# Splitting the first table load in two and spreading the decay rates by TensorE

## Chip, cores and metric

The kernel runs on one core of a Trainium2 chip, as one launch. The metric is the device time of one execution in microseconds, as a median over runs. All data are float32.

## What is computed

Two transformer blocks follow one another for one sequence of 256 tokens and width 1024. The first has a mixer of two parts (a bidirectional mLSTM and a Hyena long convolution), then a mixture of 16 experts; the second, of two layers over latent and context tokens, is not touched. The part that the change touches is the start of the first block: the modulation from `c`, the norm of `x`, and the Hyena filters with their window.

```
mod = (c @ w_ada[l] + b_ada[l])[:, None, :]
h = rms_norm(x, g_mix[l]) * (1 + sc1) + sh1
...
hid = jnp.sin(fr * (z @ w1.astype(f32) + b1.astype(f32)))
hid = jnp.sin(fr * (hid @ w2.astype(f32) + b2.astype(f32)))
h = hid @ w3.astype(f32)
window = jnp.exp(-t * jnp.abs(deltas.astype(f32))) + HYENA_WINDOW_SHIFT
return (h * window).reshape(L, HYENA_ORDER, HYENA_DIRS, HYENA_WIDTH)
```

`deltas` (the decay rates) are 2048 numbers: two orders by two directions by 512 channels. Each is the same for all 256 positions. The filters then go through a Fourier transform, are multiplied with the signal's, and come back.

## The kernel before, in words

Every engine has its own instruction stream, written out by hand in program order; semaphores join them. PE is TensorE, ACT ScalarE, DVE VectorE, POOL GpSimd, SP the engine that issues all DMAs. A stream waits where `wait_ge` stands, and what is behind waits too.

**SP and the ring.** SP issues first the small inputs (L2989 to L2991: the Hyena MLP's weights, its features, the parameter columns), then the tables `tab` (L2992, one transfer of 128 x 2878), the decay rates `dlt` (L2993, the 2048 numbers copied to all 128 partitions) and `x` (L2994). Then come the weights, by `load`, in the order of the list `stream`: slots of up to 2 MB in a ring that holds four. The first slots are `ada0` to `ada4` (parts of the modulation weights `w_ada`, issued at L3005), then `z`, `x1`, `q` and so on (parts of `w_in`). A slot's transfer waits until PE has used what lay in its place, so `ada4` waits for `ada0`. Between the fourth and the fifth slot SP issues four small transfers (L3009 to L3012), counted by `rows_loaded` (`s_row`). Semaphore `tables_loaded` (`s_load`) counts tables and rates, 16 each.

**PE at the start.** Two hidden layers of the Hyena MLP (L1287, L1291, each with a sine by ACT behind it), four filter products (L1298, 64 rows of weights by 512 columns, for order 0), one modulation slot (`ada()`, L1255: `ada0`), four filter products for order 1, the sums of the squares of `x` (L1281, from `sums`), slot `ada1`, the Fourier products of order 0 (`spectrum(0)`, L1311), slots `ada2`, `ada3` and `ada4` with the turning of the first modulation rows behind the last (L1272), `spectrum(1)`, and then the projections `z`, `x1` and so on (L1236). Results go to PSUM banks; `open_bank` takes them in turn from a ring of seven (`MIX_BANKS`) and waits until the last user of a bank has freed it.

**ACT and DVE at the start.** ACT makes the windows, `exp(-t * rate)`, eight of 128 x 512 (L1634 by way of the helper's L1605): `minus_t` is a column of `tab`, the rates are read from SBUF. DVE adds 0.05 and multiplies with the filter (L1842), then forms sum and difference of both directions (L1844, L1845). DVE frees a window for ACT by `window_used`. POOL squares `x` (L2924).

Tables, by columns of `tab`: `ident`, `ones`, then masks for the mLSTM (`tri`, `neg`), the forward Fourier tables (`dft`), the inverse ones (`idft`), 544 columns of zeros named `unused` (the place is overwritten later on), and 30 columns of small things (`minus_t`, `eps`, `pick` and others).

Of the kernel before, what the change touches and what calls it, by code (L numbers as in the profile page):

```python
# [15 lines left out]
ACT = mybir.ActivationFunctionType  # L16
# [3 lines left out]
P = 128  # L20
# [4 lines left out]
W = 512  # L25
# [13 lines left out]
MIX_BANKS, ADA_BANKS = (0, 1, 2, 3, 4, 5, 6), (7,)  # L39
# [18 lines left out]
def offsets(parts):  # L58
    at, out = 0, {}
    for name, width in parts:  # L60
# [3 lines left out]

TABLES1 = [("ident", 128), ("ones", 128), ("tri_f", 128), ("tri_b", 128), ("neg_f", 128), ("neg_b", 128),
           ("dft_c", 256), ("dft_s", 256), ("idft_c", 512), ("idft_s", 512), ("unused", 544),
           ("minus_t", 2), ("eps", 1), ("ln_eps", 1), ("pick", 8), ("token", 2), ("fold", 16)]
TABLES2 = [("half64", 128), ("flip64", 128), ("neg_col", 64), ("rope_c", 256), ("rope_s", 256),  # L70
           ("rope_r", 128), ("gla_lv", 160), ("diag32", 32), ("gla_bd", 256)]
# [91 lines left out]
def build(nc, I, out):  # L163
    ctx = ExitStack()
    with ctx:
# [7 lines left out]
        tcol, n_tab = offsets(TABLES1)  # L173
# [4 lines left out]
        tab = sb("tab", [P, n_tab])  # L178
# [17 lines left out]
        def tb(name):  # L196
            return tab[:, slice(*tcol[name])]

        ident, ones = tb("ident"), tb("ones")
# [22 lines left out]
        dlt = at(14376, 4 * W)  # L222
# [8 lines left out]
        win = [at(23600, W), at(25136, W)]  # L231
# [113 lines left out]
        def open_bank(pe, name, banks=ALL_BANKS):  # L345

            assert name not in place, name
            n = turn_of[banks] = turn_of.get(banks, -1) + 1
            b = banks[n % len(banks)]
            use = uses[b]  # L350
            uses[b] += 1
            place[name] = (b, use)
            if use:
                pe.wait_ge(free[b], use)
            return ps[b]

        def close_bank(ins, name):

            ins.then_inc(full[place[name][0]], 1)

        def read_bank(eng, name):

            b, use = place[name]
            eng.wait_ge(full[b], use + 1)
            return ps[b]
# [29 lines left out]
        s_load = sem("tables_loaded")  # L395
# [3 lines left out]
        s_row = sem("rows_loaded")  # L399
# [3 lines left out]
        hid_ready = sem("hid_ready")  # L403
        arg_ready = sem("sine_argument_ready")
        win_ready, win_used = sem("window_ready"), sem("window_used")
# [87 lines left out]
        slots, start = [{}, {}], 0  # L493
# [710 lines left out]
        def _(pe):  # L1204
            mm = nc.tensor.matmul
# [80 lines left out]
            b = open_bank(pe, "hid1", MIX_BANKS)  # L1286
# [2 lines left out]
            pe.wait_ge(hid_ready, 1)  # L1289
            b = open_bank(pe, "hid2", MIX_BANKS)  # L1290
            close_bank(mm(b[0:64, 0:T], hw2[0:64, :], hid[0:64, :], start=True, stop=True), "hid2")  # L1291
            pe.wait_ge(hid_ready, 2)
            for o in range(2):
                for n in range(TT):
                    for d in range(2):
                        j = 2 * o + d
                        b = open_bank(pe, f"filt{o}{n}{d}", MIX_BANKS)
                        close_bank(mm(b[:], hid2[0:64, P * n:P * n + P], w3[0:64, W * j:W * j + W],  # L1298
                                       start=True, stop=True), f"filt{o}{n}{d}")
                if o == 0:  # L1300
                    ada()
            pe.wait_ge(s_load, 32)
            sums("ss0", sq0, sq0_ready)
            ada()

# [72 lines left out]
            pe.wait_ge(ht_scaled, 1)  # L1378
            project("z")
            project("x1")  # L1380
            pe.wait_ge(s_row, 64)
            by_groups("gates", wg)
            w = take("q")
            fmajor("q0", w, 0, lambda k: hT[:, k, :])
# [5 lines left out]
            b = open_bank(pe, "F", MIX_BANKS)  # L1390
            for t in range(TT):
                for d in range(2):
                    o = b[:, 8 * t + 4 * d:8 * t + 4 * d + 4]
# [11 lines left out]
            for t in range(TT):  # L1405
                b = open_bank(pe, f"v{t}", MIX_BANKS)
# [16 lines left out]
            for h in range(H):  # L1423
                b = open_bank(pe, f"s{h}", MIX_BANKS)
# [4 lines left out]
            for c in range(2):  # L1429
                b = open_bank(pe, f"hss{c}", MIX_BANKS)  # L1430
# [3 lines left out]
            for d in range(2):  # L1434
                for t in range(TT):
                    for hp in range(2):
                        b = open_bank(pe, f"num{d}{t}{hp}", MIX_BANKS)
# [9 lines left out]
            for t in range(TT):  # L1447
                b = open_bank(pe, f"ym{t}", MIX_BANKS)
# [13 lines left out]
            b = open_bank(pe, "ss1", MIX_BANKS)  # L1462
# [140 lines left out]
        def act_mixers(act, step, tell):  # L1603
            def a(out_, in_, f, **kw):
                return nc.scalar.activation(out_, in_, f, **kw)  # L1605
# [17 lines left out]
            for i in range(2):  # L1623
                act.wait_ge(arg_ready, i + 1)
                step(a((hid, hid2)[i][0:64, :], hid2[0:64, :], ACT.Sin), hid_ready)
            act.wait_ge(s_load, 32)
            for o in range(2):
                for n in range(TT):
                    for d in range(2):
                        j = 2 * o + d  # L1630
                        k = (o * TT + n) * 2 + d
                        if k > 1:
                            act.wait_ge(win_used, k - 1)
                        step(a(win[d], dlt[:, W * j:W * j + W], ACT.Exp, scale=tb("minus_t")[:, n:n + 1]), win_ready)  # L1634

            def root(name, out_, n, k):
                read_bank(act, name)
# [155 lines left out]
        def dve_mixers(dve, step, tell):  # L1793
# [23 lines left out]
            for i in range(2):  # L1817
# [13 lines left out]
                if i == 0:  # L1831
                    dve.wait_ge(s_fil, 48)
                    step(v.tensor_copy(cpad[:, :, 0], pc("c", 0, 8)), c_ready)
            dve.wait_ge(s_load, 32)
            for o in range(2):
                for n in range(TT):
                    for d in range(2):
# [36 lines left out]
            tell(h_ready)  # L1874
            spectrum(1)
            T1v = T1.rearrange("p (a b) -> p a b", b=T)
            dve.wait_ge(s_row, 64)
            step(v.memset(vtok, 1.0))

            def conv(dst, src, wname, bname, m, n):  # L1880
# [1040 lines left out]
        def pool_mixers(pool, step, tell):  # L2921
            g = nc.gpsimd
            pool.wait_ge(s_x, 16)
            step(g.tensor_tensor(sq0, xT, xT, ALU.mult), sq0_ready)  # L2924
            pool.wait_ge(s_load, 32)
            for c, first in enumerate((8, 0, 4)):
                pool.wait_ge(hx_evac, c + 1)
                for m in range(first, first + 4):
                    x, y, tmp = hxc[:, m, :], hxp[:, (m + 4) % 12, :], rs
                    step(g.tensor_scalar(x, y[:, 0:T], pc("conv_hy_w", m), pc("conv_hy_b", m), ALU.mult, ALU.add))  # L2930
                    for j in (1, 2):
                        step(g.tensor_scalar(tmp, y[:, j:j + T], pc("conv_hy_w", 12 * j + m), None, ALU.mult))
                        step(g.tensor_tensor(x, x, tmp, ALU.add))
                tell(hc_ready)
# [52 lines left out]
        def _(sp):  # L2987
            for dst, src in ((hw1[0:33, :], I["hy_w1"][0]), (hfe[0:33, :], I["features"]), (hhp[0:64, 0:3], I["hy_cols"])):
                sp.dma_start(dst, src).then_inc(s_hid, 16)  # L2989
            for dst, src in ((hw2[0:64, :], I["hy_w2"][0]), (w3[0:64, :], I["hy_w3"][0]), (par[:], I["params"])):  # L2990
                sp.dma_start(dst, src).then_inc(s_fil, 16)  # L2991
            sp.dma_start(tab[:], I["tables1"]).then_inc(s_load, 16)  # L2992
            sp.dma_start(dlt, I["hy_deltas"].to_broadcast([P, 4 * W])).then_inc(s_load, 16)  # L2993
            sp.dma_start(xT, I["xT"].rearrange("(k p) t -> p k t", p=P)).then_inc(s_x, 16)  # L2994

            def load(n):
                name, src = stream[n]
                if after[n] >= 0:
                    sp.wait_ge(*freed[after[n]])
                v = slot(n, src)  # L3000
                if name[:2] == "fi":
                    for h in range(2):
                        sp.dma_start(v[:, :, 256 * h:256 * h + 256], src[:, :, h, :]).then_inc(landed[n % LANES], 16)
                else:
                    sp.dma_start(v, src).then_inc(landed[n % LANES], 16)  # L3005

            for n in range(4):
                load(n)
            sp.dma_start(bv, I["b_v"].to_broadcast([P, W])).then_inc(s_row, 16)  # L3009
            sp.dma_start(bg, I["b_gates"].to_broadcast([P, NG])).then_inc(s_row, 16)  # L3010
            sp.dma_start(wg, I["w_gates"].rearrange("p (k n) -> p k n", k=KD)).then_inc(s_row, 16)
# [98 lines left out]
```

## Time and profile before

| | us |
|---|---|
| median of 3 runs | 2252.93 (2251.94 to 2253.63) |
| profiled execution, its own time | 2251.55 |
| its span, first to last instruction | 2249.8 |
| PE busy | 2001.4 (89%) |
| DVE busy | 582.6 (26%) |
| ACT busy | 417.4 (19%) |
| POOL busy | 193.8 (9%) |

The span runs from the first to the last instruction; the execution's own time has 1.75 us around it. Granted clock of TensorE, mean of the span: 0.966. Over the span HBM is read at 294 GB/s, 661 MB in all.

### The profile page before, as it was taken

What the parts mean: (1) busy time and instruction counts of PE and PEld (TensorE: products, weight loads), DVE (VectorE), ACT (ScalarE), POOL (GpSimd) and SP (SyncE); (2) the same over time, 40 slices, a digit from 0 to 9 for tenths busy, and PEclk for the clock granted to TensorE, in tenths of its full rate; (3) what the DMA queues carried; (4) which work ended last, traced back from release to release, by engine and by line L of the source; (5) the groups of instructions that cost most, each with busy time, mean ns of one, the idle gap of its engine ahead of it and who ended that gap; (6) DMA issues with size and microseconds to landing.
All of it is one profiled execution on the core that took longest, in us unless ns stands there. A gap on an engine that the chain in (4) does not pass through costs nothing.

```text
span 2249.8 us, 32640 instructions
## 1 busy us (share of the span) xinstructions
PE 2001.4 (89%) x14140; PEld 1399.5 (62%) x14140; DVE 582.6 (26%) x1187; ACT 417.4 (19%) x766; POOL 193.8 (9%) x183
## 2 busy tenths in 40 slices
PE   7999889887788888987888887999999999999997
PEld 3856656542455545653555543756888877588886
DVE  5268220104421100000001101454432034630001
ACT  2122121202310100000000211435200033630001
POOL 0530000002000000000000000135000003600000
PEclk9999999998999999999999989999999999999999
DMA  9558899999999999999999999531487842044450
GB/s 366 207 183 332 325 420 412 408 426 417 422 393 426 427 426 424 423 420 426 424 422 426 423 378 415 146 121 36 158 297 222 201 142 88 27 150 150 126 154 19
DMA packets 181286, 664.24 MB, mean 295 GB/s; under 512 B 17335, under 2 KB 121304, under 8 KB 142552
## 3 DMA queue, kind: packets, MB, share of 16 engines
q1 hardware_dynamic: 181144, 662.15, 75.3%
q8 instruction: 112, 1.84, 0.3%
q14 instruction: 30, 0.25, 0.0%
HBM read 661.08 MB, written 1.05 MB: 294 GB/s over the span
## 4 chain that ended last, share of the span: by engine, by line
PE 47%; DMA 22%; ACT 3%; DVE 3%; issue 1%; POOL 0%; SPq 0%; ACTq 0%; DVEq 0%; POOLq 0%
PE ps L1148 19%; PE ps L650 10%; DMA ring<-in_context_weights 8%; DMA ring<-in_w_gate 7%; DMA ring<-in_w_down_slots 4%; PE ps L1532 4%; DMA ring<-in_w_up 3%; PE ps L1558 3%; PE ps L984 2%; PE ps L1157 2%; PE ps L951 2%; ACT arena L2435 1%; PE ps L846 1%; PE ps L676 1%; PE ps L1060 1%
## 5 line engine op out<-in xcount | busy, mean ns | idle before, releaser
L1148 PE MATMUL ps<-arena,ring 128*128 128x256 f32 x1984 | 429.9, 379 | 1.0 <-DVEq L389 0.9
L1148 PEld LDWEIGHTS ps<-arena,ring 128*128 128x128 f32 x1984 | 376.5, 190 | 54.2 <-issue 1.7
L1532 PE MATMUL ps<-ring,arena 128*32 128x256 f32 x4032 | 265.2, 411 | 83.8 <-DMA ring<-in_w_gate 45.3
L650 PE MATMUL ps<-arena,ring 128*128 128x256 f32 (+2 forms) x1372 | 308.2, 384 | 7.5 <-DMA ring<-in_context_weights 7.5
L650 PEld LDWEIGHTS ps<-arena,ring 128*128 128x128 f32 (+2 forms) x1372 | 248.4, 186 | 72.0 <-DMA ring<-in_context_weights 23.2
L1532 PEld LDWEIGHTS ps<-ring,arena 128*32 128x32 f32 x4032 | 128.3, 116 | 205.9 <-DMA ring<-in_w_gate 52.4
L2142 ACT ACTIVATE arena<-ps 128x512 f32<-128x512 f32 (+3 forms) x143 | 76.6, 536 | 741.0 <-PE ps L650 331.7
L1558 PE MATMUL ps<-ring,arena 128*32 128x512 f32 x1024 | 142.3, 685 | 56.9 <-DMA ring<-in_w_down_slots 50.0
L1558 PEld LDWEIGHTS ps<-ring,arena 128*32 128x32 f32 x1024 | 30.5, 120 | 155.8 <-DMA ring<-in_w_down_slots 84.0
L1236 PE MATMUL ps<-arena,ring 128*128 128x256 f32 x512 | 112.0, 380 | 1.2 <-DMA ring<-in_w_out 1.2
L2947 POOL TENSOR_TENSOR XC<-XC,arena 128x256 f32<-128x256 f32 x32 | 23.4, 730 | 988.0 <-ACT XC L2236 967.8
L1236 PEld LDWEIGHTS ps<-arena,ring 128*128 128x128 f32 x512 | 96.9, 190 | 17.2 <-issue 4.3
L2957 POOL TENSOR_SCALAR arena<-arena 128x512 f32<-128x512 f32 x48 | 78.5, 1635 | 84.2 <-DVE arena L2852 80.8
L650 PE MATMUL ps<-ring,arena 128*128 128x256 f32 (+3 forms) x312 | 85.7, 426 | 0.0
L951 PE MATMUL ps<-arena,ring 128*128 128x256 f32 x352 | 78.6, 381 | 5.3 <-DMA ring<-in_context_weights 5.3
L2606 DVE SCALAR_TENSOR_TENSOR XC<-ps,arena,XC 128x256 f32<-128x256 f32 x48 | 23.2, 484 | 225.5 <-PE ps L1148 144.3
L951 PEld LDWEIGHTS ps<-arena,ring 128*128 128x128 f32 x352 | 66.2, 190 | 20.0 <-DMA ring<-in_context_weights 9.8
L1774 ACT ACTIVATE arena<-ps 128x256 f32<-128x256 f32 x32 | 12.3, 383 | 353.6 <-PE ps L1532 353.4
L650 PEld LDWEIGHTS ps<-ring,arena 128*128 128x128 f32 x312 | 54.5, 190 | 26.9 <-issue 17.1
L2901 DVE TENSOR_TENSOR arena<-arena,ps 128x512 f32<-128x512 f32 x20 | 13.8, 688 | 212.3 <-PE ps L1148 212.3
L2111 DVE TENSOR_TENSOR arena<-arena,ps 128x256 f32<-128x256 f32 x32 | 13.5, 422 | 210.6 <-ACT arena L1774 209.4
L1255 PE MATMUL ps<-ring,arena 128*32 128x512 f32 x448 | 56.7, 633 | 11.3 <-DMA ring<-in_w_ada 10.5
(359 smaller groups left out, 1923.4 us busy)
## 6 DMA issues: line engine op xcount, KB each, us to landing
ring<-in_w_up SPq DMA_DIRECT2D x64, 2048.0 KB, 13.3
ring<-in_w_down_slots SPq DMA_DIRECT2D x64, 2048.0 KB, 14.0
ring<-in_w_gate SPq DMA_DIRECT2D x62, 2048.0 KB, 13.3
ring<-in_w_ada SPq DMA_DIRECT2D x36, 2048.0 KB, 9.8
ring<-in_w_ffn_in SPq DMA_DIRECT2D x44, 1024.0 KB, 7.6
ring<-in_context_weights SPq DMA_DIRECT2D x35, 1024.0 KB, 14.7
ring<-in_w_ffn_out SPq DMA_DIRECT2D x16, 1408.0 KB, 7.0
ring<-in_w_in SPq DMA_DIRECT2D x9, 2048.0 KB, 7.9
```

Of the source, the lines that this page charges most:

```text
L650: m = mm(o, a, x, start=(k == 0 and r == 0), stop=(k == kt - 1 and last))
L951: m = mm(b[i][:, T * x:T * x + T], w[:, k % 2, c:c + P], HID[:, k, :], start=(k == 0 and x == 0), stop=(k == 21 and x == 1))
L984: m = mm(b[:, 0:RAW], w[:, k, c:c + P], raw[:, k, :], start=(k == 0), stop=(k == KD - 1))
L1148: m = mm(b, w[:, k, c:c + P], src[:, k, :], start=(k == 0), stop=(k == kt - 1))
L1157: m = mm(b[:, 0:T], held["w"][:, k, c:c + P], oT[X][:, k, :], start=(k == 0), stop=(k == KD - 1))
L1236: m = mm(b[:, T * i:T * i + T], w[:, k, P * (j + i):P * (j + i) + P], src(k), start=(k == 0), stop=(k == ktiles - 1))
L1255: m = mm(row_bank[0][32 * g:32 * g + 32, :], cpad[:, 2 * h + k, :], w[:, k, W * g:W * g + W], start=(h == 0 and k == 0), stop=(h == 3 and ...
L1532: m = mm(b[u][32 * c:32 * c + 32, T * x:T * x + T], xs[:, 2 * h + k, CAP * e:CAP * e + CAP], w[:, k, at_:at_ + T], start=(h == 0 and k == ...
L1558: m = mm(b[a][64 * n + 32 * j:64 * n + 32 * j + 32, :], hdT[:, 2 * a + j, ch, :], w[:, j, at_:at_ + W], start=(i == 0 and odd == 0), stop= ...
L2142: step(a(dst, src, f, **kw), frees=name if frees else None)
L2947: step(nc.gpsimd.tensor_tensor(hat[st][n % 2][:, x, :], ex[st][n % 2][:, x, :], glqk[:, x, :], ALU.mult), lev_ready if x else None)
L2957: step(nc.gpsimd.tensor_scalar(Pr[n % 8], Pr[n % 8], sm[:, n % 8:n % 8 + 1], None, ALU.mult), pn_ready[X])
```

## The change

- `TABLES1` puts the forward Fourier tables right behind `ident` and `ones`, ahead of the masks.
- SP loads columns 0 to 768 (`ident`, `ones`, `dft_c`, `dft_s`) and the last 30 columns in place of the whole table, and columns 768 to 2304 (masks and inverse tables) behind the first four slots. Columns `unused` are not loaded.
- SP loads the decay rates into one partition. PE spreads them: a product of `ones[0:1, :]` (one row of weights) with the row of 512 rates fills a bank `delta0` to `delta3`. Two such products stand ahead of the filters of each order, the first two behind a wait for `tables_loaded` and ahead of the wait for the second sine.
- ACT's exponentials read the rates from the bank. The exponential of the second tile (`n` = 1) frees it.
- The waits on `tables_loaded` ask for 48 and those on `rows_loaded` for 80.

```
-TABLES1 = [("ident", 128), ("ones", 128), ("tri_f", 128), ("tri_b", 128), ("neg_f", 128), ("neg_b", 128),
-           ("dft_c", 256), ("dft_s", 256), ("idft_c", 512), ("idft_s", 512), ("unused", 544),
+TABLES1 = [("ident", 128), ("ones", 128), ("dft_c", 256), ("dft_s", 256),
+           ("tri_f", 128), ("tri_b", 128), ("neg_f", 128), ("neg_b", 128), ("idft_c", 512), ("idft_s", 512), ("unused", 544),
...
-            pe.wait_ge(hid_ready, 2)
             for o in range(2):
+                if o == 0:
+                    pe.wait_ge(s_load, 48)
+                for d in range(2):
+                    j = 2 * o + d
+                    b = open_bank(pe, f"delta{j}", MIX_BANKS)
+                    close_bank(mm(b[:], ones[0:1, :], dlt[0:1, W * j:W * j + W], start=True, stop=True), f"delta{j}")
+                if o == 0:
+                    pe.wait_ge(hid_ready, 2)
                 for n in range(TT):
...
-            pe.wait_ge(s_load, 32)
             sums("ss0", sq0, sq0_ready)
...
-            pe.wait_ge(s_row, 64)
+            pe.wait_ge(s_row, 80)
             by_groups("gates", wg)
...
-            act.wait_ge(s_load, 32)
+            act.wait_ge(s_load, 48)
...
+                        b = read_bank(act, f"delta{j}")
                         k = (o * TT + n) * 2 + d
                         if k > 1:
                             act.wait_ge(win_used, k - 1)
-                        step(a(win[d], dlt[:, W * j:W * j + W], ACT.Exp, scale=tb("minus_t")[:, n:n + 1]), win_ready)
+                        step(a(win[d], b[:], ACT.Exp, scale=tb("minus_t")[:, n:n + 1]), frees=f"delta{j}" if n else None)
+                        tell(win_ready)
...
-            sp.dma_start(tab[:], I["tables1"]).then_inc(s_load, 16)
-            sp.dma_start(dlt, I["hy_deltas"].to_broadcast([P, 4 * W])).then_inc(s_load, 16)
+            sp.dma_start(tab[:, 0:768], I["tables1"][:, 0:768]).then_inc(s_load, 16)
+            sp.dma_start(tab[:, 2848:n_tab], I["tables1"][:, 2848:n_tab]).then_inc(s_load, 16)
+            sp.dma_start(dlt[0:1, :], I["hy_deltas"]).then_inc(s_load, 16)
...
             for n in range(4):
                 load(n)
+            sp.dma_start(tab[:, 768:2304], I["tables1"][:, 768:2304]).then_inc(s_row, 16)
```

On SP, from the tables to the fifth slot, before:

```order
L2992 DMA tab<-in_tables 128x2878
L2993 DMA arena<-in_hy_deltas 128x2048
L2994 DMA XC<-in_xT 128x8x256
L3005 DMA ring<-in_w_ada 128x2x2048 x4
L3009 DMA arena<-in_b_v 128x512
L3010 DMA arena<-in_b_gates 128x16
L3011 DMA arena<-in_w_gates 128x256
L3012 DMA arena<-in_w_router 128x256
L3005 DMA ring<-in_w_ada 128x2x2048 [waits slots_drained]
```

and in the changed kernel:

```order
L3000 DMA tab<-in_tables 128x768
L3001 DMA tab<-in_tables 128x30
L3002 DMA arena<-in_hy_deltas 1x2048
L3003 DMA XC<-in_xT 128x8x256
L3014 DMA ring<-in_w_ada 128x2x2048 x4
L3018 DMA tab<-in_tables 128x1536
L3019 DMA arena<-in_b_v 128x512
L3020 DMA arena<-in_b_gates 128x16
L3021 DMA arena<-in_w_gates 128x256
L3022 DMA arena<-in_w_router 128x256
L3014 DMA ring<-in_w_ada 128x2x2048 [waits slots_drained]
```

One transfer of 2878 columns has become three of 768, 30 and 1536, the last of them behind four slots, and the rates have one row.

On PE, behind the hidden layers (`ps0` to `ps7` are the banks; `ps7` holds modulation rows), before:

```order
L1298 MATMUL ps2<-arena 128x512 [waits hid_ready]
L1298 MATMUL ps3<-arena 128x512
L1298 MATMUL ps4<-arena 128x512
L1298 MATMUL ps5<-arena 128x512
L1255 MATMUL ps7<-ring,arena 32x512 [waits landed0,c_ready]
L1255 MATMUL ps7<-ring,arena 32x512 x7
L1298 MATMUL ps6<-arena 128x512
L1298 MATMUL ps0<-arena 128x512 [waits free0]
L1298 MATMUL ps1<-arena 128x512 [waits free1]
L1298 MATMUL ps2<-arena 128x512 [waits free2]
L1281 MATMUL ps3<-arena,tab 128x256 [waits free3,x_squares_ready,tables_loaded]
```

and in the changed kernel, where L1298 is the product with the rates and L1305 the filter's:

```order
L1298 MATMUL ps2<-arena,tab 128x512 [waits tables_loaded]
L1298 MATMUL ps3<-arena,tab 128x512
L1305 MATMUL ps4<-arena 128x512 [waits hid_ready]
L1305 MATMUL ps5<-arena 128x512
L1305 MATMUL ps6<-arena 128x512
L1305 MATMUL ps0<-arena 128x512 [waits free0]
L1255 MATMUL ps7<-ring,arena 32x512 [waits landed0,c_ready]
L1255 MATMUL ps7<-ring,arena 32x512 x7
L1298 MATMUL ps1<-arena,tab 128x512 [waits free1]
L1298 MATMUL ps2<-arena,tab 128x512 [waits free2]
L1305 MATMUL ps3<-arena 128x512 [waits free3]
L1305 MATMUL ps4<-arena 128x512 [waits free4]
```

The wait for the tables has moved from behind both filter groups to ahead of the first, and all banks behind are four places on.

## Rows read from the trace of the kernel before

**Rows 1.** The page: the strip of transfer rates in 40 slices, and the chain's shares.

```profile
GB/s 366 207 183 332 325 420 412 408 426 417 422 393 426 427 426 424 423 420 426 424 422 426 423 378 415 146 121 36 158 297 222 201 142 88 27 150 150 126 154 19
...
PE 47%; DMA 22%; ACT 3%; DVE 3%; issue 1%; POOL 0%; SPq 0%; ACTq 0%; DVEq 0%; POOLq 0%
```

**Rows 2.** Timeline of PE: start, duration, engine, line, operation, count, idle time ahead and releaser.

```profile
13.43 7.19 PE L1298 MATMUL ps<-arena 64*128 64x512 f32 x8 [3.83 <-ACT arena L1605]
23.45 3.57 PE L1255 MATMUL ps<-ring,arena 128*32 128x512 f32 x16 [2.83 <-DMA ring<-in_w_ada]
26.95 3.70 PE L1298 MATMUL ps<-arena 64*128 64x512 f32 x8
30.58 3.72 PE L1281 MATMUL ps<-arena,tab 128*128 128x256 f32 x16
...
39.71 3.64 PE L1255 MATMUL ps<-ring,arena 128*32 128x512 f32 x32
45.74 1.92 PE L1255 MATMUL ps<-ring,arena 128*32 128x512 f32 x16 [2.39 <-DMA ring<-in_w_ada]
...
48.51 3.68 PE L1311 MATMUL ps<-arena,tab 128*128 128x512 f32 x8
52.03 27.79 PE L1236 MATMUL ps<-arena,ring 128*128 128x256 f32 x128
```

**Rows 3.** Stretches: length, busy time of five engines, granted clock, DMA share, GB/s.

```profile
5.00:13.00 8.00, 1.08 (x2) 0.29 (x2) 5.78 (x17) 0.45 (x2) 0.00 (x0) 1.00 1.00 352
5.00:23.40 18.40, 8.27 (x10) 2.76 (x10) 11.06 (x22) 5.01 (x7) 3.60 (x1) 1.00 1.02 382
20.00:25.00 5.00, 2.17 (x9) 0.46 (x12) 4.63 (x4) 0.89 (x2) 2.02 (x1) 1.00 1.02 424
5.00:45.00 40.00, 28.17 (x106) 10.60 (x106) 27.17 (x46) 11.45 (x16) 3.60 (x1) 1.00 1.02 397
65.00:80.00 15.00, 15.00 (x75) 12.88 (x77) 0.00 (x0) 1.99 (x5) 11.35 (x15) 1.00 0.40 143
```

**Rows 4.** DMA issues of the first 90 us: count, KB each, us from issue to landing.

```profile
tab<-in_tables SPq DMA_DIRECT2D x1, 1439.0 KB, 8.8
arena<-in_hy_deltas SPq DMA_DIRECT2D x1, 1024.0 KB, 10.9
...
arena<-in_hy_w SPq DMA_DIRECT2D x1, 16.0 KB, 2.1
```

**Rows 5.** Timeline of PE, ACT, DVE and SP (SPq is its queue) in the first 35 us.

```profile
4.07 0.43 SPq L2992 DMA_DIRECT2D tab<-in_tables  x1
...
8.52 1.08 PE L1291 MATMUL ps<-arena 64*64 64x256 f32 x2 [3.91 <-ACT arena L1605]
...
12.96 0.42 ACT L1605 ACTIVATE arena<-arena 64x256 f32<-64x256 f32 x1 [4.59 <-DVE arena L1830]
...
18.54 0.72 ACT L1605 ACTIVATE arena<-arena,tab 128x512 f32<-128x512 f32 x1 [0.21 <-DVEq L389]
...
33.82 0.69 DVE L1845 TENSOR_TENSOR arena<-arena 128x512 f32<-128x512 f32 x1
```

**Rows 6.** What SP waited for up to 312 us, the two largest: us, times, longest.

```profile
SPq L3005 <- PE ps L1236: 117.6, 8, 17.9
SPq L3005 <- PE ps L1255: 95.0, 26, 12.1
```

**Rows 7.** Timeline of PE late in the mixers and at the first experts.

```profile
228.13 1.94 PE L1450 MATMUL ps<-tab,arena 128*128 128x128 f32 x8 [2.90 <-DVE arena L2032]
230.00 2.70 PE L1255 MATMUL ps<-ring,arena 128*32 128x512 f32 x16
...
275.50 3.21 PE L1255 MATMUL ps<-ring,arena 128*32 128x512 f32 x16 [2.13 <-DMA ring<-in_w_ada]
...
305.94 3.66 PE L1532 MATMUL ps<-arena 128*32 128x256 f32 x64 [0.69 <-ACT arena L1760]
...
313.57 3.57 PE L1532 MATMUL ps<-ring,arena 128*32 128x256 f32 x32 [2.24 <-DMA ring<-in_w_gate]
```

More of the change, by code:

```diff
@@ L1833, in dve_mixers @@
                     step(v.tensor_copy(cpad[:, :, 0], pc("c", 0, 8)), c_ready)
-            dve.wait_ge(s_load, 32)
+            dve.wait_ge(s_load, 48)
             for o in range(2):
@@ L1876, in dve_mixers @@
             T1v = T1.rearrange("p (a b) -> p a b", b=T)
-            dve.wait_ge(s_row, 64)
+            dve.wait_ge(s_row, 80)
             step(v.memset(vtok, 1.0))
@@ L2924, in pool_mixers @@
             step(g.tensor_tensor(sq0, xT, xT, ALU.mult), sq0_ready)
-            pool.wait_ge(s_load, 32)
+            pool.wait_ge(s_load, 48)
             for c, first in enumerate((8, 0, 4)):
```

## The prediction

> **What bounds the kernel now.** I read the page first. Of the chain that ended last, PE holds 47% and DMA 22% [rows 1]. Its strip of transfer rates starts low, holds above 320 GB/s from the fifth slice and falls to 183 to 207 GB/s in the second and third, so no single limit holds over the whole span. The change lies in the first 50 us, and each later stage has to be asked whether it passes a shift on.
>
> PE in order of time comes next [rows 2]. From 13.43 us PE is busy except for two waits for modulation weights: 2.83 us ahead of 23.45 (slot ada0) and 2.39 us ahead of 45.74 (slot ada4). The projections that carry the mixers begin at 52.03. The same rows show two speeds: eight instructions of the filter product take 7.19 us at 13.43 and 3.70 us at 26.95, a modulation slot 3.57 us and then 1.92 us. The granted clock is 1.00 in these stretches [rows 3], yet by the durations TensorE runs at 1.2 GHz until about the end of ada0's slot and at 2.4 GHz behind it.
>
> The third view is the transfers. From 5 to 45 us the DMA share is 1.02 at 397 GB/s [rows 3]: the queue never drains, so when a slot lands is a matter of the bytes ahead of it. Ahead of ada0 stand tables of 1439 KB and decay rates of 1024 KB [rows 4].
>
> Behind 65 us the queue has room (143 GB/s, share 0.40, with PE at 15.00 of 15.00 us) [rows 3], and in the first 312 us SP waits 213 us for two kinds of PE's work, the projections and the modulation slots, to free places [rows 6]. There the transfers follow PE. A shift of PE at 52 us is thus handed on, through transfers that are issued earlier by as much.
>
> **The transfers, costed.** Ahead of ada4 the change takes away the 127 copies of the rates (1016 KB) and the 544 unused columns (272 KB). The 1536 moved columns (768 KB) stay ahead of it, since the later part is issued behind four slots and ada4 is the fifth. That is 1288 KB, or 1.32 MB; at 397 GB/s it is 3.3 us, so ada4 lands 3.3 us earlier and can start at 42.4. At the slowest and fastest rate of rows 3 that fits, 352 and 424 GB/s, it is 3.7 and 3.1 us. Ahead of ada0 the 768 KB go too: 2.1 MB, 5.5 us at 382 GB/s, and ada0 lands near 17.9.
>
> When does PE have what its new wait asks for? The tables landed 8.8 us after their issue at 4.07, at 12.87 [rows 4, 5]. In their place of 1439 KB now stand 407 KB, rates included, and 1032 KB less at 352 GB/s [rows 3] is 3.0 us: 9.9 us. Bounds: not before 7.1, from the new issue of the rates near 5.0 and the 2.1 us in which a 16 KB transfer landed; not after 12.87, where the whole table landed. I take 9.9 since the stretch is bound by bytes. The small transfers are the doubtful part. A 16 KB one landed in 2.1 us, with more work behind it [rows 4], so I add nothing for two of them. The Trainium skill, DMA: Bandwidth & Descriptors, section Bandwidth, speaks against such cuts: transfers under 64 KB are bound by descriptors and a 4 KB one keeps the engines 0.68 us. By that page, estimated, the two would take some 1.3 us from the gain, and the sum would be 2.0 us and not 3.3.
>
> **PE, costed.** Two banks of rates are multiplied ahead of the first four filters: four instructions, half of the eight at 7.19 us, 3.6 us. They fill the idle time between the second hidden layer (its product starts at 8.52 and lasts 1.08 [rows 5]) and the sine at 12.96, which ends at 13.38. From 9.9 they end at 13.5 where the filters started at 13.43: +0.1. With the landing at 12.87 it would be +3.0, ada0 would start at 23.65, and 0.3 us would be left of the whole gain. PE reads one row of weights here against 64 there; I see no reason for another time, since the columns are the same.
>
> The filters end at 20.7, ada0 has landed at 17.9, and the wait of 2.83 goes: ada0 starts at 20.7 and not at 23.45, -2.75. It runs at the lower clock as before (3.5 us to the next start). Then come two banks of rates, half of 3.70: +1.85. The second filters so start at 26.05 and not at 26.95: -0.9. The squares' sums, ada1, the first spectrum, ada2 and ada3 follow without a wait, as before, and end at 42.45 for 43.35. ada4 then starts at the later of PE (42.45) and its landing (42.4): 3.3 us earlier than 45.74. The two limits meet, so neither alone could give more. Turning the modulation, the second spectrum and the projections follow at their old distances: z starts at 48.7.
>
> Costed at nothing, each with its cover. The exponentials now read a bank and free it: before they read SBUF at 722 ns each, and the combining work of DVE, 2.9 us a pair, ends at 34.51 [rows 5] while the second spectrum asks for it at 48.51. That is 14 us of cover; without it a longer exponential would show eight times over. The four more banks turn the ring of seven by four places. The frees that PE waits for at its start are the third exponential's (ended at 19.26 [rows 5], asked for near 25) and, from 26 on, those of the first filters, whose readers had been through by then before and start earlier now. The second table part is wanted at 79.75 by the gates and at 55.6 by DVE behind its second spectrum, and is ahead of ada4, in place by 42. One more issue on SP ahead of the slots costs 0.43 us [rows 5] against a queue that is never empty: nothing. The squares of x on POOL start earlier, and PE wants them no sooner than 29.6.
>
> **Sum:** -0.9 - 2.4 = -3.3 us at the projections, and by rows 6 the same at the end. The profiled execution took 2251.55 us (2249.8 of span and 1.75 around it); against it 2248.25. It stands 1.38 below the median of 2252.93. From the median I get 2249.6. A measurement of this kernel tells about 0.2%, 4.5 us, from no change, so this gain, real as it may be, would lie inside.
>
> **Rivals.** (a) The clock comes up during the filters, since PE is now at work from 9.9 without a gap. Then the filters and ada0 shorten by 3.5 + 1.65 us, ada0 waits for its landing again, and PE reaches ada4 near 38, four us ahead of its landing. The gain stays capped at 3.3, and the long wait can put the clock back: behind waits of 2.13 and 2.90 us slots took 3.21 and 2.70 us against 1.92 [rows 7]. That gives back 1 to 3 us: 2251.6. Against it: 7.19 us of filters did not bring the clock up before. The Trainium skill, TensorE: Matmul & The Clock Gate, Part 1, has the clock rise with sustained matmul work and fall when PE idles. By that rule (a) is what to expect; the first filters of this trace do not agree, and the slots behind the waits do.
>
> (b) The clock stays down longer. The rates use one row, the filters 64, and neither kind brought it up; they now follow ada0 directly for 5.5 us. If 1.2 GHz lasts through the second rates, filters and sums, that adds 1.85 + 3.5 + 3.7 = 9.0 us. PE would come to ada4 at 51.5, 5.7 us later than 45.74: 2258.6, slower. It decides from 3.3 us of added PE time on. Against it: the clock rose inside ada0's own slot, which is the same work in the same order still, and 64-row filters behind it ran fast.
>
> (c) The gain is lost behind. Seen for it: PE waits for transfers at 275.50 and 313.57 [rows 7], and whatever is bound by bytes alone from a fixed moment on does not move. Against it: those transfers are issued when PE frees slots. No change: 2252.9. That the change would not do what it says can be ruled out by the order: the rates are one row, and the tables two pieces.
>
> (d) More than 4.5 us. Clock losses behind waits, 0.8 us at 230.00, 1.3 at 275.50 and 1.7 at 313.57 [rows 7], are a matter of phase. With a start 3.3 us earlier, half of them may go. Besides, the first expert slot waits 0.69 us for ACT at 305.94, where it opens the bank of the last gathered tokens; the turned ring gives it banks that were free before. 2247.5.
>
> **How the numbers follow.** Forecast 0.62 (its own range, from the landing at 12.87 at one end, -0.3, and 3.7 us from the rates of transfer with 0.7 of phase at the other, is 2248.5 to 2252.6); (a) 0.08, (b) 0.06, (c) 0.08, (d) 0.16. The range 2246.3 to 2253.0 takes in (a), (c), the forecast and most of (d); (b) and the far end of (d) stay out. Faster by over 0.2%: (d) and a tail of 0.04 of the forecast, 0.2. Slower: (b), 0.06. The rest, 0.74, is within.
>
> **What would show it.** Right: the first new product on PE near 9.9 and ended by 13.5; the first filter at 13.4 to 13.6 (landing at 12.87: near 16.4); no wait for ada0, which starts near 20.7 at 3.5 us; the second filters near 26; no wait, or under 0.5 us, ahead of ada4 near 42.4; z near 48.7; and every later milestone, the first expert product at 305.94 above all, earlier by 3.3. Wrong: filters of 3.7 us ahead of ada0 (a), sums of 7 us (b), z early and 305.94 unmoved (c), or slots of 1.92 us at 230, 275 and 313 (d).

## The result and the profile after

| | before | after |
|---|---|---|
| median, us | 2253.28 (20 runs, 2250.43 to 2263.29) | 2261.0 (20 runs, 2255.74 to 2271.4) |
| span of the profiled execution | 2249.8 | 2260.5 |
| projections start (z) | 52.03 | 60.33 |

The ratio is 1.0029 (95% interval 1.0020 to 1.0039): slower by 4.5 to 8.8 us, where 3.3 us less had been forecast. The time lies outside the range of 2246.3 to 2253.0.

The page of the changed kernel, the strip of transfer rates and the chain's shares, as [rows 1]:

```profile
GB/s 309 219 168 310 325 423 424 401 427 422 408 391 428 426 427 424 424 419 426 424 422 428 424 384 415 121 149 21 167 297 226 193 146 79 36 144 154 126 154 19
...
PE 46%; DMA 22%; DVE 4%; ACT 3%; issue 1%; POOL 0%; SPq 0%; ACTq 0%; DVEq 0%; POOLq 0%
```

The first slice of 56 us moved less (309 for 366 GB/s), and the rest has its old shape. The loss is at the start. The timeline of PE there, as [rows 2]; L1298 is now the product with the rates and L1305 the filters':

```profile
9.65 3.78 PE L1298 MATMUL ps<-arena,tab 1*128 1x512 f32 x4
16.92 7.19 PE L1305 MATMUL ps<-arena 64*128 64x512 f32 x8 [3.49 <-ACT arena L1611]
24.04 3.64 PE L1255 MATMUL ps<-ring,arena 128*32 128x512 f32 x16
27.61 3.78 PE L1298 MATMUL ps<-arena,tab 1*128 1x512 f32 x4
31.31 7.19 PE L1305 MATMUL ps<-arena 64*128 64x512 f32 x8
38.44 5.68 PE L1281 MATMUL ps<-arena,tab 128*128 128x256 f32 x16
44.04 1.92 PE L1255 MATMUL ps<-ring,arena 128*32 128x512 f32 x16
45.90 3.70 PE L1317 MATMUL ps<-arena,tab 128*128 128x512 f32 x8
49.53 3.64 PE L1255 MATMUL ps<-ring,arena 128*32 128x512 f32 x32
54.04 1.93 PE L1255 MATMUL ps<-ring,arena 128*32 128x512 f32 x16 [0.87 <-ACT arena L1611]
...
60.33 27.79 PE L1236 MATMUL ps<-arena,ring 128*128 128x256 f32 x128
```

Two things are to be seen, and a third that is not there. The first filters start 3.49 us late, for ACT. From the first rates to the middle of the sums every product runs at the lower level, 1.2 GHz, by its duration: second rates 3.78 us (1.85 expected), second filters 7.19 for 3.70, sums 5.68 for 3.72. And neither ada0 nor ada4 waits for its transfer. Against [rows 2] the start of each step is off by: filters +3.49, ada0 +0.59 (its old wait of 2.83 took most of it up), second filters +4.36, sums +7.86, ada2 +9.82, ada4 +8.30, z +8.30.

Why was ACT late? The timeline of DVE, POOL and ACT in the changed kernel, with the step ahead of each sine (L1838):

```profile
7.76 0.28 DVE L1838 TENSOR_SCALAR arena<-arena 64x256 f32<-64x256 f32 x1
...
12.60 3.60 POOL L2932 TENSOR_TENSOR arena<-XC 128x2048 f32<-128x2048 f32 x1 [12.18 <-DMA XC<-in_xT]
12.70 3.65 DVE L1838 TENSOR_SCALAR arena<-arena 64x256 f32<-64x256 f32 x1
...
16.45 0.42 ACT L1611 ACTIVATE arena<-arena 64x256 f32<-64x256 f32 x1 [7.96 <-DVE arena L1838]
```

x has landed by 12.6, near 6 us earlier than before, and POOL squares it at once. DVE's last step ahead of the second sine starts 0.1 us later and takes 3.65 us for 0.28: it ends at 16.35, 0.15 us behind the end of POOL's (16.20). The kernel before had the same encounter elsewhere, seen in the same view of its own trace:

```profile
18.42 3.60 POOL L2924 TENSOR_TENSOR arena<-XC 128x2048 f32<-128x2048 f32 x1 [18.00 <-DMA XC<-in_xT]
...
18.60 0.69 DVE L1842 SCALAR_TENSOR_TENSOR arena<-arena,ps 128x512 f32<-128x512 f32 x1 [0.21 <-DVE arena L1842]
19.43 3.13 DVE L1844 TENSOR_TENSOR arena<-arena 128x512 f32<-128x512 f32 x1
```

There it held a step that had 14 us of cover. The Trainium skill, SBUF — State Buffer, section Who interferes with whom, says that a DVE operation in a two-port mode, or one with two inputs in SBUF against a GpSimd operation that reads SBUF, shares a port pair with GpSimd as an exclusive lock, and the second to come blocks until the first is done. Both traces agree: the DVE step came second, and took 3.65 us for 0.28 and 3.13 us for 0.69.

The waits for transfers are gone, as forecast. Stretches of the changed kernel, as [rows 3]:

```profile
5.00:45.00 40.00, 32.87 (x70) 12.89 (x74) 20.50 (x34) 9.37 (x13) 3.60 (x1) 1.00 0.89 345
40.00:45.00 5.00, 5.00 (x26) 3.40 (x28) 0.96 (x3) 0.47 (x1) 0.00 (x0) 1.00 0.00 0
65.00:80.00 15.00, 15.00 (x72) 13.19 (x71) 0.00 (x0) 1.90 (x4) 3.88 (x6) 1.00 0.57 216
```

The queue is even empty from 40 to 45 us (0 GB/s): SP waits 17.9 us for PE to free a place and issues the next slot, z, at 46.03 (36.21 before), so the limit has passed from the transfers to PE. Later, as [rows 7]:

```profile
237.87 3.16 PE L1255 MATMUL ps<-ring,arena 128*32 128x512 f32 x16
...
283.89 2.81 PE L1255 MATMUL ps<-ring,arena 128*32 128x512 f32 x16 [2.22 <-DMA ring<-in_w_ada]
...
316.29 3.66 PE L1538 MATMUL ps<-arena 128*32 128x256 f32 x64
...
321.87 1.93 PE L1538 MATMUL ps<-ring,arena 128*32 128x256 f32 x32 [0.19 <-DMA ring<-in_w_gate]
```

The first expert product is 10.35 us late, of which 2 us arise behind 301.68, where it was still 8.40: PE waits 1.96 us for DVE there and not 0.86, and two groups of products take 3.26 and 6.55 us for 2.56 and 5.66; a little later, where PE had waited for a transfer before, the lateness is 8.30 again (321.87 for 313.57).

### The profile page after: what moved, and what is told of

It reads as the page before. It is cut to its first block, busy times and chain, and to the rows that moved or that the text cites. A ratio compares the mean times of both kernels' runs of the same rounds, so it can differ in the third digit from the quotient of the medians.

```text
span 2260.5 us, 32665 instructions
## 1 busy us (share of the span) xinstructions
PE 2023.3 (90%) x14148; PEld 1411.8 (62%) x14148; DVE 583.5 (26%) x1187; ACT 417.1 (18%) x766; POOL 193.9 (9%) x183
## 4 chain that ended last, share of the span: by engine, by line
PE 46%; DMA 22%; DVE 4%; ACT 3%; issue 1%; POOL 0%; SPq 0%; ACTq 0%; DVEq 0%; POOLq 0%
PE ps L1148 19%; PE ps L650 9%; DMA ring<-in_context_weights 8%; DMA ring<-in_w_gate 6%; DMA ring<-in_w_down_slots 5%; PE ps L1538 4%; DMA ring<-in_w_up 2%; PE ps L1564 2%; PE ps L984 2%; PE ps L1157 2%; PE ps L951 2%; ACT arena L2443 1%; PE ps L846 1%; PE ps L676 1%; PE ps L1577 1%
```

## The experiments

All timings, each with a ratio to runs of the kernel before that were taken beside it on the same chip. "z" is the start of the projections in the profiled execution of that kernel. Where one run stands, there is no interval, and its time is not used.

| kernel | z, us | ratio, 95% interval |
|---|---|---|
| changed | 60.33 | 1.0029 (1.0020 to 1.0039) |
| pool_later | 54.18 | 1.0020 (1.0006 to 1.0035) |
| sums_first | 54.01 | 1.0011 (0.9998 to 1.0023) |
| both_mended | 50.83 | 1.0008 (0.9996 to 1.0020) |
| x_early_before | 51.14 | one run, 2254.97 us |
| tables_alone | 53.95 | 0.9996 (0.9985 to 1.0008) |
| rates_alone | 60.06 | 1.0032 (1.0015 to 1.0048) |
| row_products_before | 57.42 | one run, 2257.22 us |
| row_products_timed | 56.22 | 1.0018 (1.0008 to 1.0028) |
| rates_128_rows | 49.78 | one run, 2253.41 us |
| rates_128_timed | 49.59 | 1.0006 (0.9992 to 1.0019) |
| rates_128_alone | 52.51 | 1.0012 (1.0002 to 1.0022) |
| fifth_slot_first | 47.56 | 0.9999 (0.9986 to 1.0011) |

### POOL's squares, later

```
             pool.wait_ge(s_x, 16)
+            pool.wait_ge(hid_ready, 2)
             step(g.tensor_tensor(sq0, xT, xT, ALU.mult), sq0_ready)
```

> The changed kernel, but POOL squares x only once the second sine is done. Theory 1 (POOL's squares held up DVE's last step ahead of the sine, 3.65 us for 0.28, and so the filters): that step takes 0.28 us again, the filters start at 13.5 for 16.92, and if the clock behaves as in the changed kernel everything behind is 3.4 us earlier, z at 56.9, some 3.4 us less than the changed kernel, still 3 to 5 us more than before. Rival (the second sine is late for another reason, such as the new products on PE): the filters stay near 16.9 and the time near that of the changed kernel.

The timeline of PE, and DVE's step, in pool_later:

```profile
12.57 0.29 DVE L1838 TENSOR_SCALAR arena<-arena 64x256 f32<-64x256 f32 x1
...
13.43 7.19 PE L1305 MATMUL ps<-arena 64*128 64x512 f32 x8
20.55 3.20 PE L1255 MATMUL ps<-ring,arena 128*32 128x512 f32 x16
23.68 1.98 PE L1298 MATMUL ps<-arena,tab 1*128 1x512 f32 x4
25.59 6.24 PE L1305 MATMUL ps<-arena 64*128 64x512 f32 x8
31.76 6.21 PE L1281 MATMUL ps<-arena,tab 128*128 128x256 f32 x16
```

The step is back at 0.29 us and the filters at 13.43, so theory 1 stands for the 3.49 us. Of z 6.15 us came back and not 3.4, since the clock behaved otherwise: it rose within ada0 (3.20), stayed up for the second rates (1.98) and fell again in the second filters (6.24 for 3.70; granted clock 0.58 from 25.6 to 31.7). So the rates' place costs even when ada0 has brought the clock up. Where the clock rises varies by trace: both_mended, below, has the same work up to the end of ada0, and there ada0 took 3.64. The median is 4.5 us above before (1.4 to 7.9), within the 3 to 5 expected.

### Sums and ada1 ahead of the second rates

```
                 if o == 0:
                     ada()
+                    sums("ss0", sq0, sq0_ready)
+                    ada()
-            sums("ss0", sq0, sq0_ready)
-            ada()
```

ACT's root of the sums moves between its two groups of exponentials.

> The changed kernel, but on PE the sums of squares and slot ada1 stand directly behind ada0, and rates and filters of order 1 behind them (ACT takes the root between its two groups of exponentials). Theory 2 (the clock stays at 1.2 GHz because 1-row and 64-row products follow ada0): the clock rises within ada0 or the sums, the second rates take 1.9 us and the second filters 3.7; from the start of ada0 to the first spectrum 12 to 15 us for 21.9; z near 53 to 55 for 60.33, 5 to 7 us less than the changed kernel. Rival (the clock rises at some late moment whatever PE works on): second filters at 7.19 us again, and no gain.

The timeline of PE in sums_first:

```profile
23.84 3.64 PE L1255 MATMUL ps<-ring,arena 128*32 128x512 f32 x16
27.41 3.86 PE L1281 MATMUL ps<-arena,tab 128*128 128x256 f32 x16
31.19 1.92 PE L1255 MATMUL ps<-ring,arena 128*32 128x512 f32 x16
33.05 1.98 PE L1298 MATMUL ps<-arena,tab 1*128 1x512 f32 x4
34.96 3.70 PE L1305 MATMUL ps<-arena 64*128 64x512 f32 x8
```

The same instructions, in another order, take 14.7 us from ada0 to the first spectrum (38.58) for 21.9. What follows ada0 decides, so theory 2 stands in that and its rival falls. But 1-row and 64-row products do not take the clock down wherever they stand: behind the sums and ada1, 5.5 us of them ran at the upper level here, while in pool_later, behind ada0 alone, the clock fell in them. No run shows what makes this difference. By the ratios the time is some 4 us less than the changed kernel's, where 5 to 7 had been expected.

### Both mended

> Both edits together. Theories 1 and 2 add up: filters at 13.5, z near 50 to 51.5, bounded by the landing of ada4 near 42; 8 to 10 us less than the changed kernel, 1 to 3 us less than before (2250 to 2252). If only theory 1 holds, 3.4 us less than the changed kernel; if only theory 2, 5 to 7 less.

z at 50.83, as expected, 9.5 us ahead of the changed kernel and 1.2 ahead of before. The time is within noise of before (interval -0.9 to +4.5 us), where 1 to 3 us less had been expected; by the ratios it is some 5 us less than the changed kernel's, where 8 to 10 had been expected.

### x ahead of the tables, in the kernel before

```
+            sp.dma_start(xT, I["xT"].rearrange("(k p) t -> p k t", p=P)).then_inc(s_x, 16)
             sp.dma_start(tab[:], I["tables1"]).then_inc(s_load, 16)
             sp.dma_start(dlt, I["hy_deltas"].to_broadcast([P, 4 * W])).then_inc(s_load, 16)
-            sp.dma_start(xT, I["xT"].rearrange("(k p) t -> p k t", p=P)).then_inc(s_x, 16)
```

> The kernel before with x issued ahead of tables and rates, nothing else. Theory 1: x lands near 11.5, POOL's 3.6 us of squares fall on DVE's steps ahead of the second sine (11.22 to 12.86), one of them takes over 2 us, and the filters start near 15 to 16 for 13.43, with no product of rates on PE at all. The time hardly moves, since ada0's slot lands at 23.4 as before. Rival: DVE's steps keep their 0.28 us and the filters 13.43.

The timeline of POOL, DVE and PE in x_early_before:

```profile
12.46 3.60 POOL L2924 TENSOR_TENSOR arena<-XC 128x2048 f32<-128x2048 f32 x1 [12.03 <-DMA XC<-in_xT]
12.58 3.62 DVE L1830 TENSOR_SCALAR arena<-arena 64x256 f32<-64x256 f32 x1
...
16.77 7.19 PE L1298 MATMUL ps<-arena 64*128 64x512 f32 x8 [7.17 <-ACT arena L1605]
23.89 3.44 PE L1255 MATMUL ps<-ring,arena 128*32 128x512 f32 x16
27.25 3.70 PE L1298 MATMUL ps<-arena 64*128 64x512 f32 x8
```

The encounter is made by x's landing alone, with no rates on PE. At ada0 it costs 0.4 us only, since ada0 had been late anyway; z even comes 0.9 us earlier, since ada4 starts at 44.86 for 45.74 with the same bytes ahead of it. Landings differ by about 1 us between traces without a change of bytes. And the clock is up for the second filters though ada0 follows the first ones without a gap: it is not the missing gap that keeps it down.

### The two halves of the change

tables_alone is the kernel before with the new order of columns, the waits' counts to match, and

```
-            sp.dma_start(tab[:], I["tables1"]).then_inc(s_load, 16)
+            sp.dma_start(tab[:, 0:768], I["tables1"][:, 0:768]).then_inc(s_load, 16)
+            sp.dma_start(tab[:, 2848:n_tab], I["tables1"][:, 2848:n_tab]).then_inc(s_load, 16)
...
+            sp.dma_start(tab[:, 768:2304], I["tables1"][:, 768:2304]).then_inc(s_row, 16)
```

> The kernel before with the tables in two parts and nothing else: the rates stay 128 copies in SBUF, PE has no product with them. Account of the transfers: ada4 lands 0.7 us earlier (272 KB), ada0 2.7 us earlier, near 20.8; x near 15.6, too late to meet DVE's steps ahead of the second sine, so filters at 13.43. PE starts ada0 near 20.8, the clock rises in it or soon after, z at 51.3 (-0.7). By theory 2 the filters alone (64 rows) do not keep the clock down, since they did not in the kernel before; the second filters take 3.7 us. Rival (any start of ada0 directly behind the filters keeps the clock down): second filters 7.2 us, z 52 to 53.

The timeline of PE in tables_alone:

```profile
20.61 3.64 PE L1255 MATMUL ps<-ring,arena 128*32 128x512 f32 x16
24.18 4.19 PE L1298 MATMUL ps<-arena 64*128 64x512 f32 x8
...
44.35 2.37 PE L1255 MATMUL ps<-ring,arena 128*32 128x512 f32 x16 [3.27 <-DMA ring<-in_w_ada]
...
48.38 5.73 PE L1311 MATMUL ps<-arena,tab 128*128 128x512 f32 x8
```

PE ran ahead as expected, and the second filters behind it took 4.19 us and not 7.2, so the rival falls. ada4 started 1.39 us earlier (0.7 by its bytes), and PE had waited 3.27 us for it. Behind that wait the clock was down (granted clock 0.50 from 46 to 52): slot 2.37 for 1.92, spectrum 5.73 for 3.68, z 1.9 us late and not 0.7 early. The time did not move.

rates_alone is the changed kernel with the whole table in one transfer.

> The changed kernel with the whole table in one transfer ahead of the rates. The tables land near 12.9, so the first rates run from 12.9 to 16.6, filters from 16.7 to 23.9, without any held-up step on DVE (x lands near 15.8). Theory 2: the clock stays at 1.2 GHz through ada0, second rates, second filters and part of the sums, as in the changed kernel, and z comes at 58 to 60. Rival: the clock rises in ada0 and z comes near 53 to 54. If so, the split of the tables is needed for the loss.

The timeline of PE in rates_alone:

```profile
27.29 3.78 PE L1298 MATMUL ps<-arena,tab 1*128 1x512 f32 x4
30.99 7.19 PE L1305 MATMUL ps<-arena 64*128 64x512 f32 x8
38.12 5.72 PE L1281 MATMUL ps<-arena,tab 128*128 128x256 f32 x16
```

The whole loss is here, z at 60.06 and 1.0032, without the split and without DVE's held step (its last step takes 0.28 us; the filters start at 16.59 because the rates land later, at 12.88). The rates on PE are what costs.

### Two 1-row products in the kernel before

```
                         b = open_bank(pe, f"filt{o}{n}{d}", MIX_BANKS)
+                        if o == 1 and n == 0:
+                            if d == 0:
+                                pe.wait_ge(s_load, 32)
+                            mm(b[:], ones[0:1, :], dlt[0:1, W * j:W * j + W], start=True, stop=True)
```

> The kernel before with two 1-row products of 512 columns (four instructions) between ada0 and the second filters, into banks that the filters then overwrite; nothing reads them. Nothing else moves: filters at 13.43, ada0 at 23.45. Their bare cost is 1.9 us and would be swallowed by the wait of 2.39 ahead of ada4: z at 52.0 to 52.5. Theory 2: the clock falls back to 1.2 GHz, or does not rise, behind ada0, the second filters take 5 to 7.2 us and the sums over 4: z 3 to 5 us later than 52.03. Rival: the products cost only their 1.9 us.

The timeline of PE in row_products_before:

```profile
23.23 3.41 PE L1255 MATMUL ps<-ring,arena 128*32 128x512 f32 x16 [2.60 <-DMA ring<-in_w_ada]
...
29.72 5.49 PE L1302 MATMUL ps<-arena 64*128 64x512 f32 x6
35.14 6.07 PE L1281 MATMUL ps<-arena,tab 128*128 128x256 f32 x16
```

Four instructions with no reader bring second filters and sums down: six filter instructions take 5.49 us, near 0.9 each, for 0.46 at the upper level (eight in 3.70), and the granted clock reads 0.50 from 30 to 35 us. z is 5.4 us late where their bare 1.9 us would mostly have been swallowed.

> The kernel before with the two 1-row products behind ada0, timed. In the one look z came at 57.42, 5.4 us late, by the clock alone. If a later z is handed on to the end, the median is 4 to 6 us above before (1.0018 to 1.0027). If the stage behind 310 us, bound by transfers, takes a shift up, it is 0 to 2 us.

Timed, 1.0018: slower by 1.8 to 6.3 us, with z 4.2 late in its trace. This is nearly the clock's share by itself, measured in time: by estimate, the bare 1.9 us and the 0.87 us for ACT's copy ahead of ada4 exceed the old wait of 2.39 by only 0.4 us.

### The rates over 128 rows

On pool_later, with POOL zeroing the other 127 rows first and SP waiting for that ahead of the rates' transfer:

```
-                    close_bank(mm(b[:], ones[0:1, :], dlt[0:1, W * j:W * j + W], start=True, stop=True), f"delta{j}")
+                    close_bank(mm(b[:], ones, dlt[:, W * j:W * j + W], start=True, stop=True), f"delta{j}")
```

> pool_later with the rates' products over all 128 rows (the other 127 rows of the rates' place are zeroed by POOL at the start, so the result is the same). The columns and so the bare times are the same. If the number of rows at work is what matters, the first rates themselves or ada0 bring the clock up and it stays up: second rates 1.9 us, second filters 3.7, sums 3.7, z near 50 to 51. If the rows do not matter (or zeros do not count), the times are those of pool_later: second filters over 5 us, sums over 5.

The timeline of PE in rates_128_rows:

```profile
9.60 3.78 PE L1298 MATMUL ps<-arena,tab 128*128 128x512 f32 x4
13.45 4.12 PE L1305 MATMUL ps<-arena 64*128 64x512 f32 x8
17.50 1.92 PE L1255 MATMUL ps<-ring,arena 128*32 128x512 f32 x16
...
21.27 3.70 PE L1305 MATMUL ps<-arena 64*128 64x512 f32 x8
...
42.01 3.41 PE L1255 MATMUL ps<-ring,arena 128*32 128x512 f32 x16 [4.34 <-DMA ring<-in_w_ada]
```

The same columns and the same result, and the clock is up before the first filters are through: 4.12 us for 7.19. ada4's landing bounds now, at 42.01 (42.4 in the forecast), and behind the wait for it the granted clock reads 0.50 from 42 to 45 us.

> rates_128_rows again, timed. With both causes gone (POOL later, clock up before the first filters) z comes at 49.8 by the one look at it, 2.3 us earlier than before: 0 to 3 us less than the kernel before by its median, and 5 to 10 less than the changed kernel measured beside its own before (ratio 1.0029). If the clock's rise in that look was a chance of phase, z and the filters vary and the median comes out near that of pool_later, 1.002 of before.

A second trace has the same times (filters 4.05, z 49.59), so it was no chance. The median is 1.0006 (-1.8 to +4.3 us), unclear against before, where 0 to 3 us less had been expected; pool_later, with one row in place of 128, had 1.0020.

> The changed kernel with the rates' products over all 128 rows and POOL's squares left where the change put them. Theory 1 and 2 as found: DVE's last step is held for 3.6 us and the filters start at 16.7; PE waits 3.4 us ahead of them. If the clock is up by then it may stay up or fall: filters 3.7 to 7.2. From there at the upper level, z 49.8 if only ada4's landing near 42 bounds it, 52 if the filters are slow. Time between rates_128_timed (1.0006) and 1.001.

Without POOL's wait the filters start at 16.82 and run at the lower level (7.19); from the second rates on all is at the upper one. z comes at 52.51, 2.9 us behind rates_128_timed, and 1.0012.

In all 14 traces the second filters go the same way. Where 1-row products stand directly behind ada0 (changed, pool_later, rates_alone and both of the row products) eight instructions took 6.24 to 7.19 us, or six of them 5.48 to 5.49; in the nine others eight took 3.70 to 4.19.

### The fifth slot ahead of the later tables

On rates_128_rows; the second table part and the four small loads move behind the fifth slot.

```
-            for n in range(4):
+            for n in range(5):
                 load(n)
             sp.dma_start(tab[:, 768:2304], I["tables1"][:, 768:2304]).then_inc(s_row, 16)
```

> The same, with the second table part and the four small loads issued behind the fifth slot instead of the fourth. ada4 is what PE waits for there (4.34 us); 1.3 MB less ahead of it is 3.2 us: it lands near 38.9, z near 46.6, the wait near 1.2 us. If a shift of z reaches the end, 3 us less than rates_128_timed and 3 to 6 less than before (ratio 0.998). Rival (what is won at z is lost behind it, in the waits for transfers and the clock between 210 and 320 us): z at 46.6 and the median that of rates_128_timed.

The timeline of PE in fifth_slot_first:

```profile
38.53 1.92 PE L1255 MATMUL ps<-ring,arena 128*32 128x512 f32 x16 [0.89 <-DMA ring<-in_w_ada]
...
47.56 8.66 PE L1236 MATMUL ps<-arena,ring 128*128 128x256 f32 x39 [2.58 <-DMA ring<-in_w_in]
```

ada4 starts at 38.53, but PE now waits 2.58 us for the next slot, z, whose transfer is issued behind the moved loads; z comes at 47.56 and not at 46.6, 2.0 us ahead of rates_128_timed. The median is 0.9999 (-3.2 to +2.5 us). No version beat the kernel before.

What becomes of a shift at z? In the traces it is intact at the output projections (229.60 for 233.92 in fifth_slot_first, 242.22 in the changed kernel). From the tokens' gathering on (L1499 in before, L1505 here, x96) to the second block (L984) the stage bound by transfers follows, and its length scatters: 1400.84 - 317.08 = 1083.8 us in before, 1403.5 - 311.03 = 1092.5 in fifth_slot_first, 1412.59 - 323.73 = 1088.9 in the changed kernel. Over all 14 traces it runs from 1083.8 to 1094.1 us, in no order by z: 1092.5 also in pool_later (z 54.18), 1090.0 in x_early_before (51.14), 1085.3 in tables_alone (53.95). The one trace of before is the shortest of all, so the end of a single trace says nothing of a shift of a few us; the medians have to. By them leads at z of 1.2, 2.4 and 4.5 us (both_mended, rates_128_timed, fifth_slot_first) went unseen, while lags of 4.2 and 8.3 us (row_products_timed, changed) were seen, at 1.8 to 6.3 and 4.5 to 8.8. What takes a lead up stays open.

## Why the prediction was wrong, point by point

- **"The clock rose inside ada0's own slot, which is the same work in the same order still"** is the step that failed. It was the argument against rival (b), which then came true with a chance of 0.06. Rates, filters and sums cost 1.93 + 3.49 + 1.96 = 7.4 us more than at the upper level (9.0 in the rival), and z came 8.3 late (5.7). ada0 took 3.64 us, so the clock did not rise in it at all; before it had risen only at the very end of the slot (3.57). The order of ada0 and the filters was the same; the rates between them were not, and two such products suffice (row_products_before).
- **How the sum missed**: z was forecast at 48.7 and came at 60.33, 11.6 us later. ada0 started at 24.04 for 20.7 (3.3, DVE's held step), the clock took 7.4, and ACT's copy ahead of ada4 0.9.
- **"PE reads one row of weights here against 64 there; I see no reason for another time"**: right for the first products themselves (3.78 for 3.6), wrong for what comes behind ada0.
- **"The squares of x on POOL start earlier"**, costed at nothing, is the second failed step, and no rival held it. I had asked when PE wants the squares and not what POOL's 3.6 us meet on DVE. It cost 3.49 us at the filters. By the forecast's own rates x lands near 13, and DVE's steps end at 12.9: that was within its error, and the 3.13 us of L1844 stood in the trace. By pool_later against the changed kernel, 6.15 us of z hang on it together with the clock's phase.
- **The landing of the rates at 9.9**: no later than that. The products start at 9.65, directly behind the second hidden layer, as in every trace with this load, so the landing itself is not seen. The rule of the Trainium skill, DMA: Bandwidth & Descriptors, section Bandwidth, on small transfers, estimated at 1.3 us, did not show: the first product would have started near 11.2.
- **ada0 without a wait**: right. **ada4's landing at 42.4**: in the changed kernel it was issued at 27.74 and landed 13.0 us later, at 40.7. With the same bytes ahead it landed at 40.5 to 40.7 where the next slot was issued at 33.18 or later, and at 41.7 to 42.0 where that was issued near 30 (both_mended, rates_128_rows, rates_128_timed). The sum counted the bytes ahead of a slot only. It was off by up to 1.9 us and decided nothing here, for PE came later still.
- **"No wait, or under 0.5 us, ahead of ada4"**: off, it was 0.87. The slot asks for bank 7, which ACT must have copied first (53.30 to 53.90); the wait of 2.39 before had covered that. Of the forecast 3.3 us only 2.4 were to be had without moving more.
- **Rival (a)**, that PE runs ahead, waits for ada4 and loses its clock: seen in tables_alone (wait 3.27, then 5.73 for 3.68) and rates_128_rows (wait 4.34, then 3.41 for 1.92), not in the changed kernel. The rule of the Trainium skill, TensorE: Matmul & The Clock Gate, Part 1, that I had weighed as favouring it (the clock rises with sustained matmul work) did not hold for the mix here, 64-row products, ada0, 1-row and 64-row products: in the changed kernel PE was at work from 16.92 to past 38.44 without a gap, and the level stayed low.
- **The strip "holds above 320 GB/s from the fifth slice"** up to the 25th only; the last 15 slices lie between 19 and 297. Nothing in the sum hangs on it.
- **A shift of PE at 52 us is handed on**: right for the lag, within its interval. For a lead it was not confirmed.
- **"4.5 us from no change"**: the 20 runs of before lie between 2250.43 and 2263.29, those of the changed kernel between 2255.74 and 2271.4; with 20 of each, 6.5 us stood clear of no change.

## What to carry to other kernels

When work is moved onto an idle engine, ask what it does to the clock of what stands behind it: a few products of one row, directly behind ada0, cost 3.8 us by themselves and 5.4 more in the filters and sums. Behind the sums and ada1 the same ones cost 2.0 and nothing more. When a transfer comes earlier, so does every engine's work that it releases, and each must be placed against what the others do at that time; that a stall is hidden today says nothing of the next place it falls. And a lead won at one wait is worth what the next wait leaves of it, so find that one first.

## What was not expected of the hardware

- Filling 128 rows in place of 1, 127 of them zeros, left the product's time as it was or a little less (3.54 to 3.78 us for four instructions) and brought the first filters from 7.19 to 4.12, 4.05 and, in fifth_slot_first, 3.70 us. In rates_128_alone, where PE waited 3.65 us in between, they took 7.19. With 1-row products ahead they stayed at 7.19 in every trace (changed, pool_later, sums_first, both_mended, rates_alone).
- The granted clock reads 1.00 from 5 to 45 us in the changed kernel, where durations double and halve. In this stretch the level had to be read from the durations, not from that column. Later falls do show in it: 0.50 from 30 to 35 us in row_products_before and from 42 to 45 in rates_128_rows.
- A DVE step with one of its two inputs in PSUM ran beside POOL's squares at its usual 0.69 us (18.60 in the kernel before), while the two steps with all inputs in SBUF that met them took 3.13 and 3.65 us.
